# A two-block transformer on one core: expert retrieval merged with 42 down products, modulation sums turned to rows, compression with stationary blocks

## What is computed

```python
m  = (silu(c)     @ w_mod[l] + b_mod[l]).reshape(B, 9, 1024)     # tokens
mc = (silu(c_ctx) @ w_mod[l] + b_mod[l]).reshape(1, 9, 1024)     # context
x  = x + 0.5 * m[:, 2] * swiglu(mod_norm(x, m, 0, g), w1, w2)    # and the same for the 256 context tokens
...
```

```python
return gelu(blk @ w1 + b1) @ w2          # blk: 30 rows of 2048, w1: 2048 x 256
```

```python
q = (h @ w_q).reshape(B, TB, 8, 2, 128)              # 8 heads, 2 halves
s = einsum('btphd,phnd->btphn', q, subkeys)          # 128 subkeys each
v, i = top_k(s, 16)                                  # per head and half
cand = v[..., 0, :, None] + v[..., 1, None, :]       # 256 pair sums
tv, tj = top_k(cand, 16)                             # 16 experts a head
eidx = take_along_axis(cidx, tj);  w = softmax(tv)
a = gelu(einsum('btd,btpkd->btpk', hblk, w_down[eidx]))
return einsum('btpk,btpkd->btd', w * a, w_up[eidx])  # of 128 x 128 experts
```

## Time and profile before

| | |
|---|---|
| time, median of 3 runs | 3140.7 us (3140.38 to 3141.37) |
| the profiled execution | 3140.06 us |
| its span | 3138.3 us |
| granted TensorE clock, mean | 0.952 |
| PE / DVE / ACT / POOL busy | 2926.0 (93%) / 2188.5 (70%) / 1230.2 (39%) / 368.8 us (12%) |
| DMA | 450 MB, 143 GB/s over the span |

### The profile page before, as it was taken

One profiled execution on the slowest core, in us unless ns is written; L12 is line 12 of the kernel. 1 busy time (PEld: TensorE's weight loads), 2 busy tenths in 40 slices (PEclk: granted clock), 3 DMA queues, 4 the chain that ended last, 5 costly groups with the idle time before them and its releaser, 6 DMA issues. The chain is left out here.

```text
span 3138.3 us, 47109 instructions
## 1 busy us (share of the span) xinstructions
PE 2926.0 (93%) x16182; PEld 2491.5 (79%) x16182; DVE 2188.5 (70%) x4187; ACT 1230.2 (39%) x2276; POOL 368.8 (12%) x412
## 2 busy tenths in 40 slices
PE   7999999999999999999999997688379999999998
PEld 4888888568888888888859996568268999999997
DVE  2888894558888975657556664455998777777775
ACT  2322233443222332223455454154025454444454
POOL 0111115000111100100400000000375000000000
PEclk9999999999999999999999998689559999999999
DMA  5555442123544454534415556004002555555553
GB/s 230 175 174 192 171 146 94 41 101 132 190 175 169 148 200 148 174 132 159 130 36 170 185 173 229 1 27 149 1 0 73 186 186 186 186 187 186 187 187 120
DMA packets 107708, 450.01 MB, mean 143 GB/s; under 512 B 11953, under 2 KB 12593, under 8 KB 94257
## 3 DMA queue, kind: packets, MB, share of 16 engines
q1 hardware_dynamic: 93744, 347.46, 34.3%
q0 software_dynamic: 13824, 100.67, 8.5%
HBM read 447.04 MB, written 1.05 MB: 143 GB/s over the span
## 5 line engine op out<-in xcount | busy, mean ns | idle before, releaser
L177 DVE TENSOR_TENSOR weight_lo<-weight_ring,weight_hi 128x512 fp32r<-128x512 f32 x1272 | 942.0, 746 | 553.6 <-ACT weight_hi L170 539.1
L170 ACT ACTIVATE weight_hi<-weight_ring 128x512 fp32r<-128x512 f32 x1272 | 798.6, 631 | 1204.8 <-PE bank L256 1203.5
L254 PE MATMUL bank<-operand_hi,weight_hi 128*128 128x256 f32 (+1 forms) x3168 | 1042.7, 329 | 24.0 <-DVE operand_lo L591 12.9
L256 PE MATMUL bank<-operand_hi,weight_lo 128*128 128x256 f32 (+1 forms) x3168 | 1035.7, 327 | 0.0
L255 PE MATMUL bank<-operand_lo,weight_hi 128*128 128x256 f32 (+1 forms) x3168 | 1035.6, 327 | 0.0
L254 PEld LDWEIGHTS bank<-operand_hi,weight_hi 128*128 128x128 f32 x3168 | 604.0, 191 | 89.0 <-issue 21.4
L255 PEld LDWEIGHTS bank<-operand_lo,weight_hi 128*128 128x128 f32 x3168 | 604.2, 191 | 53.8
L256 PEld LDWEIGHTS bank<-operand_hi,weight_lo 128*128 128x128 f32 x3168 | 604.1, 191 | 51.2
L846 DVE SCALAR_TENSOR_TENSOR extension_ffn<-extension_ffn,silu_c 128x512 f32<-128x512 f32 x532 | 392.9, 788 | 1.7
L254 PE MATMUL bank<-hidden_hi_ffn,weight_hi 128*128 128x512 f32 (+1 forms) x704 | 258.5, 367 | 2.0 <-DVE arena L1071 1.9
L256 PE MATMUL bank<-hidden_hi_ffn,weight_lo 128*128 128x512 f32 (+1 forms) x704 | 255.7, 363 | 0.0
(11 more groups left out here) (253 smaller groups left out, 2934.3 us busy)
## 6 DMA issues: line engine op xcount, KB each, us to landing
weight_ring<-in_ffn SPq DMA_DIRECT2D x272, 512.0 KB, 3.6
weight_ring<-in_experts SPq DMA_DIRECT2D x256, 512.0 KB, 3.5
extension_ffn<-in_w_mods POOLq DMA_DIRECT2D x96, 1024.0 KB, 7.1
weight_ring<-in_w_mix SPq DMA_DIRECT2D x56, 512.0 KB, 3.6
weight_ring<-in_w_second SPq DMA_DIRECT2D x52, 512.0 KB, 3.9
extension_mixer<-in_rel_bias SPq DMA_DIRECT2D x2, 1536.0 KB, 6.7
arena<-in_x SPq DMA_DIRECT2D x1, 2048.0 KB, 9.2
arena<-in_cmp_k SPq DMA_DIRECT2D x1, 2048.0 KB, 11.6
```

What stands on the lines that cost most here:

```text
L170: nc.scalar.activation(self.hi[:, g % 2, h], self.ring[:, g % NS, h], ACT.Copy).then_inc(self.rounded, 1)
L177: self.nc.vector.tensor_tensor(self.lo[:, g % 2, h], self.ring[:, g % NS, h], self.hi[:, g % 2, h].bitcast(F32), ALU.subtract).then_inc(se ...
L254: nc.tensor.matmul(out, a_hi, b_hi, start=start and n == 0, stop=False)
L256: last = nc.tensor.matmul(out, a_lo, b_hi, start=False, stop=stop and n == len(pairs) - 1)
```

## The change

Three parts.

1. **Modulation sums in rows.** The accumulated tile now moves (512 columns), and the stationary operand is a window of 32 columns of `pick`, a matrix of zeros with one column of ones: the window's place decides in which of 32 rows of the bank the sum comes. At the end ScalarE copies the rows (`move`), TensorE transposes them in four pieces (`turn`), VectorE collects. Collecting and `finish` now stand behind the last product's VectorE work.
2. **Compression.** The 30 columns of the blocks are stationary and `w1` moves (256 columns), 32 fp32 matmuls; the result is copied, transposed and goes through gelu as before.
3. **Retrieval.** `Scores` and `stage_retrieve` become one class `Retrieve`, which also takes 42 down units (`K0`). The top 16 of a head begin when its scores are there. The tables are made for four tokens at a time (`BATCH`): VectorE's `compare` makes both tables in one instruction (128 x 4 x 2 x 128), GpSimd's `weigh` multiplies the first by the weights, `spread` is four matmuls, `keep` one copy of 128x512. `beside_down` places the batches: none in the first 19 units (`ALONE`), one per half unit in units 19 to 34, two per half in 35 to 41, four behind. The weights' subtraction is GpSimd's throughout this class (`subtract_beside`). The gelu of the 42 units is stored to device memory (`spill`) by SP's queue, and loaded again in `Experts`, whose order has 86 down units, and an up unit of a stored gelu after every second of the others and at the end.

```diff
+    def subtract_beside(self, pool, j, halves=(0, 1)):
+        g = self.g0 + j
+        for i in halves:
+            pool.wait_ge(self.rounded, 2 * g + i + 1)
+            h = slice(i * HALF, (i + 1) * HALF)
+            self.nc.gpsimd.tensor_tensor(self.lo[:, g % 2, h], self.ring[:, g % NS, h], self.hi[:, g % 2, h].bitcast(F32),
+                                         ALU.subtract).then_inc(self.split, 1)
...
         pe.wait_ge(self.halved.sem, self.halved.at(d + 1))
-        for n in range(self.blocks):
-            at = 2 * self.blocks * d + 2 * n
-            out = c.bank[6 + (d < self.early)][:, at:at + 2]
-            b = slice(n * P, (n + 1) * P)
-            nc.tensor.matmul(out, self.hi[:, b], c.ones_r[:, :], start=True, stop=False)
-            last = nc.tensor.matmul(out, self.lo[:, b], c.ones_r[:, :], start=False, stop=True)
+        for g in range(self.groups):
+            row = self.groups * d + g
+            pick = self.pick[:, ROWS - 1 - row:2 * ROWS - 1 - row]
+            out = c.bank[6 + (d < self.early)][0:ROWS, :]
+            final = d in (self.early - 1, self.n - 1) and g == self.groups - 1
+            nc.tensor.matmul(out, pick, self.hi[:, g * 512:(g + 1) * 512], start=(d in (0, self.early) and g == 0), stop=False)
+            last = nc.tensor.matmul(out, pick, self.lo[:, g * 512:(g + 1) * 512], start=False, stop=final)
         last.then_inc(self.summed.sem, 1)
...
             for n in range(2):
-                for m in range(2):
-                    for j in range(16):
-                        mm = nc.tensor.matmul(chip.bank[2 * n + m][:, 0:2 * NCB], w1[n][:, j, m * P:(m + 1) * P],
-                                              blk[n][:, j, :], start=(j == 0), stop=(j == 15))
-                    mm.then_inc(chip.product.sem, 1)
+                for j in range(16):
+                    mm = nc.tensor.matmul(chip.bank[n][0:2 * NCB, 0:256], blk[n][:, j, :], w1[n][:, j, :],
+                                          start=(j == 0), stop=(j == 15))
+                mm.then_inc(chip.product.sem, 1)
...
+NQ, K0 = 16, 42
+ALONE = 19
+TURN_AT, EXP_AT = [(ALONE - 1, 1), (ALONE + 14, 0)], [(ALONE - 2, 1), (ALONE + 13, 0)]
+LEFT = (P // BATCH + 4 * (K0 - ALONE - 16), S // BATCH)
...
+        def spread(b):
+            if b >= 4:
+                pe.wait_ge(self.kept.sem, self.kept.at(b - 3))
+            pe.wait_ge(self.weighted.sem, self.weighted.at(b + 1))
+            hots = self.hots(b)
+            for j in range(BATCH):
+                mm = nc.tensor.matmul(chip.bank[4 + b % 4][:, j * NK:(j + 1) * NK], hots[:, j, 0, :], hots[:, j, 1, :],
+                                      start=True, stop=True)
+            mm.then_inc(self.spread.sem, 1)
...
+        for i in range(K0):
+            if i < 2:
+                pe.wait_ge(self.evicted.sem, self.evicted.at(NQ - 1 + i))
+            else:
+                pe.wait_ge(self.gelu_done.sem, self.gelu_done.at(i - 1))
+            for half in range(2):
+                units.half_chunk(pe, NQ + i, half, chip.bank[i % 2][:, 0:S], x)
+                if i == 0 and half == 0:
+                    score(PH - 1)
+                for b in beside_down(i, half):
+                    spread(b)
+                if (i, half) == TURN_AT[1]:
+                    turn(1)
+            if (i, 1) == TURN_AT[0]:
+                turn(0)
...
+        for i in range(K0):
+            units.round(act, 0, NQ + i + 2, [0])
...
+            for b in beside_down(i, 0):
+                keep(b)
...
+            units.round(act, 0, NQ + i + 2, [1])
+            act.wait_ge(units.used, units.used_at(NQ + i))
+            if i >= 4:
+                act.wait_ge(chip.spilled[i % 4], 16 * (i // 4))
+            nc.scalar.activation(self.f[i % 4], chip.bank[i % 2][:, 0:S], ACT.Gelu_apprx_tanh).then_inc(self.gelu_done.sem, 1)
+            for b in beside_down(i, 1):
+                keep(b)
...
+        def weigh(b):
+            pool.wait_ge(self.compared.sem, self.compared.at(b + 1))
+            a = self.hots(b)[:, :, 0, :]
+            w = self.columns[:, 2, BATCH * b:BATCH * (b + 1)].unsqueeze(2).to_broadcast([P, BATCH, P])
+            nc.gpsimd.tensor_tensor(a, a, w, ALU.mult).then_inc(self.weighted.sem, 1)
+
+        for n in range(NQ):
+            units.subtract_beside(pool, n + 2)
+        for i in range(K0):
+            for half in range(2):
+                units.subtract_beside(pool, NQ + i + 2, [half])
+                for b in beside_down(i, half):
+                    weigh(b)
...
+def expert_order():
+    seq, early = [("down", K0), ("down", K0 + 1)], 0
+    for k in range(K0, NK):
+        seq.append(("up", k))
+        if k + 2 < NK:
+            seq.append(("down", k + 2))
+        if (k - K0) % 2 and early < K0:
+            seq.append(("up", early))
+            early += 1
+    return seq + [("up", k) for k in range(early, K0)]
...
-            run(nc, [add, Scores(chip, stream, add.then)])
-            stage_retrieve(chip)
-            stage_experts(chip, stream)
+            run(nc, [add, retrieve, Experts(chip, stream, retrieve)])
```

More of the change, by code:

```diff
@@ L790, in __init__ @@
         self.stepped = chip.mod_step.take(self.steps * self.n)
+        self.pick, self.rows = chip.extra["pick"], chip.part(A_RSTD, 512)[0:ROWS]
+        self.moved, self.turned = (s.take(1 + (early > 0)) for s in (chip.mod_moved, chip.mod_turned))
         self.rounded, self.halved, self.summed = (s.take(self.n) for s in (chip.mod_rounded, chip.mod_split, chip.mod_summed))
@@ new lines, in sum, with move, turn @@
+        last.then_inc(self.summed.sem, 1)
+    def move(self, act, upto):
+        c, nc = self.chip, self.chip.nc
+        act.wait_ge(self.summed.sem, self.summed.at(upto))
+        nc.scalar.activation(self.rows[:, :], c.bank[6 + (upto == self.early)][0:ROWS, :], ACT.Copy).then_inc(self.moved.sem, 1)
+    def turn(self, pe, upto):
+        c, nc = self.chip, self.chip.nc
+        pe.wait_ge(self.moved.sem, self.moved.at(1 if upto == self.early or not self.early else 2))
+        for k in range(4):
+            last = nc.tensor.transpose(c.bank[6 + (upto == self.early)][:, k * ROWS:(k + 1) * ROWS],
+                                       self.rows[:, k * P:(k + 1) * P], c.ident[0:ROWS, 0:ROWS])
+        last.then_inc(self.turned.sem, 1)
@@ L986, in tensor @@
                     work.sum(pe, d - 1)
+            if self.gate_first and n0 == 0:
+                work.turn(pe, work.early)
             for n in range(KT):
@@ L1001, in tensor @@
                     work.sum(pe, d - 1)
+        if work:
+            work.turn(pe, work.n)
     def scalar(self, act):
@@ L1019, in scalar @@
                     work.round(act, d - 1)
+                if self.gate_first and n0 == 0 and u == 13:
+                    work.move(act, work.early)
             if n0 + nh == FT:
@@ L1444, with beside_down @@
 E_HOT = E_WORK + 3 * S
-HOTS = 8
-B_WORDS = E_HOT + HOTS * 2 * P
+BATCH = 4
+B_WORDS = E_HOT + 2 * BATCH * 2 * P
+NQ, K0 = 16, 42
+ALONE = 19
+TURN_AT, EXP_AT = [(ALONE - 1, 1), (ALONE + 14, 0)], [(ALONE - 2, 1), (ALONE + 13, 0)]
+LEFT = (P // BATCH + 4 * (K0 - ALONE - 16), S // BATCH)
+def beside_down(i, half):
+    n = i - ALONE
+    if n < 0:
+        return range(0)
+    if n < 16:
+        return range(2 * n + half, 2 * n + half + 1)
+    first = P // BATCH + 4 * (n - 16) + 2 * half
+    return range(first, first + 2)
 class Proj:
@@ new lines, in __init__, with hots @@
+        n = S // BATCH
+        self.compared, self.weighted, self.spread, self.kept = (
+            x.take(n) for x in (chip.hot0, chip.hot1, chip.spread, chip.kept))
+        self.weight, self.columns = chip.part(0, S, NK), chip.part(E_SLOT, 3, S)
+        self.slots = chip.part(E_N, 3, SLOTS)
+        self.f = [chip.extra["early"][:, i, :] for i in range(4)]
+    def hots(self, b):
+        per = BATCH * 2 * P
+        at = b % 6 if b < S // BATCH - 8 else b % 2
+        if at < 2:
+            base = E_HOT + per * at
+        else:
+            base = (E_SC if b < P // BATCH else S * NK - 4 * per) + per * (at - 2)
+        return self.chip.part(base, BATCH, 2, P)
@@ L1894, in tensor @@
     def tensor(self, pe):
-        chip, nc, units, q, keys = self.chip, self.chip.nc, self.units, self.q, self.keys
+        chip, nc, units, r = self.chip, self.chip.nc, self.units, self.retrieve
         x = lambda kt: (self.hi[:, kt, :], self.lo[:, kt, :])
-        self.norm.sums(pe)
-        self.norm.spread(pe)
-        units.pair(pe, [chip.bank[0][:, 0:S], chip.bank[6][:, 0:S]], x, self.norm.split_in)
-        for n in range(2, 16):
-            k = n // 2
-            if n >= 4 and n % 2 == 0:
-                pe.wait_ge(self.evicted.sem, self.evicted.at(k - 1))
-            units.chunk(pe, 0, n, chip.bank[k % 2][:, n % 2 * S:(n % 2 + 1) * S], x)
@@ new lines, in tensor @@
+        pe.wait_ge(r.gelu_done.sem, r.gelu_done.at(K0))
+        pe.wait_ge(r.kept.sem, r.kept.at(S // BATCH))
+        w = 0
```

(13 more changed lines are left out.)

624 lines of the change are left out of this document (319 added, 305 removed).

## The result

| | before | changed |
|---|---|---|
| time, median | 3141.0 us (3140.4 to 3142.9, 4 runs) | 3220.1 us (3218.2 to 3222.3, 4 runs) |
| ratio, 95% interval | | 1.0251 (1.0233 to 1.0269) |
| the profiled execution, its span | 3140.1, 3138.3 us | 3220.8, 3219.0 us |
| granted TensorE clock, mean | 0.952 | 0.951 |

The change is 2.5% slower; 3213 us was forecast. Both early parts gain what they should, and the retrieval gives back more than that.

What follows compares the result with a forecast made beforehand. TensorE was taken to bound the feed-forward layers, waits between engines the rebuilt retrieval. 3140.1 + 112 (retrieval) - 28 (modulation sums) - 10.5 (compression) - 1 (block boundary) = 3212.6 us, 2.3% slower; range 3130 to 3245.

Steps and rivals of the forecast that it cites:

- Modulation sums: Feed-forward layers: 152 matmuls of 512 columns replace 608 of 2, gain 28 us, bounds 15 and 30.
- The deduction for VectorE's room: Modulation sums: 28 us taken of a 29.8 us gain, because VectorE has a little less room under the shorter cover.
- Compression: 32 matmuls with 256 moving columns replace 64 with 30: 17 us in place of 27.5, gain 10.5.
- The start of the region: From the first query product: TensorE waits 10 us, to 118; first comparison, weighting and copy end at 121 us.
- the ring: Units 19 to 34: half chunk, rounding, subtraction, weighting and spread follow without overlap, 6.1 us per half at full clock, 8.0 low.
- The clock: In the retrieval's loop: three halves of four at the low level, making 497 us from 427 at full clock.
- Region: First query product to first expert product behind the retrieval: 497 us, against 385 before, a cost of 112 us.
- Moved for nothing: 42 stores and loads on SP's queue and 42 early up units among the later units: no cost.
- the full clock through the ring: Rival: the full clock holds in the loop, region 427 us, 3142 us in all, no change; 10 in 100.
- The one in which the engines' sums count: Rival: GpSimd and its shared interface bound the halves, region 364, 3080 us; within the faster share, 16 in 100.

Runs made afterwards that it cites:

- the part alone: The kernel before with only the modulation sums in rows: 3110.9 us, ratio 0.9903 of before.
- 10.0 alone: The kernel before with only the compression part of the change: 3129.9 us, ratio 0.9965 of before.
- the dense run: The changed kernel with 12 unread fp32 matmuls on TensorE before each half unit's spread, from unit 20 on: 3166.5 us, ratio 1.0087 of before.
- the opened ring: The changed kernel with GpSimd's weighting of a half unit's batches before its subtraction: 3064.0 us, ratio 0.9759 of before.

## Why the prediction was right

By its own steps:

- **Modulation sums**: 28 taken, bound 30; the trace shows 30.4, the part alone 29.3. The deduction for VectorE's room was not needed, and the part gave what its matmuls alone were summed to, 29.8.
- **Compression**: 10.5 taken, 10.8 in the trace, 10.0 alone.
- **The start of the region**: TensorE's wait before the transposes was put at 10 us, to 118 us after the first query product, and is 11.66, to 122.7; the units before it took 111 us for 108, 1.5 of it behind a subtraction of GpSimd. The first batch was to be through at 121; its comparison began at 124.1 (2213.76), and its spread at 131.2 (2220.86), because GpSimd's first weighting already stands behind a subtraction that waits for TensorE: the ring begins one half unit earlier than it was counted.
- **The ring**: named with its edges, and each edge is in the timeline. At the full clock 6.1 us was summed, 5.75 is measured with TensorE kept dense. The term that was too long is GpSimd's weighting, taken at 1.30 from the subtraction's row, measured at 1.04. The estimate that the prediction set beside it from the Trainium skill's page GPSIMD Engine Reference, 1.1 us, is the nearer one for the weighting, and too low for the subtraction, 1.26. At the low clock 8.0 was summed; in this kernel's loop a half with one batch mostly lasts 6.9 to 7.8 us, with both levels in it, and 7.8 where the clock was nearest to low (0.51 to 0.55); six of the 32 last 8.4 to 9.3, and in each of these GpSimd's subtraction or weighting shows longer, beside VectorE's work.
- **The clock**: three halves of four at the low level were taken, a granted clock near 0.6. It was 0.69 to 0.72 in the halves with one spread and 0.80 to 0.81 in those with two. The first 32 halves took 243 us where 241 follow from the prediction, the 14 with two spreads 106 where 128 do; that is the term that was mis-sized, together with the last batches (11 us for 7). It comes from the second weighting, which costs 1.0 us by itself and in part runs beside the spread of the first, and from the higher clock.
- **Region**: 497 forecast, 487.1 measured. By its terms: 6 us more before the first half of the ring (127 for 121), 3 more in the halves with one spread, 22 less in those with two, 4 more at the end.
- **Moved for nothing**: the stores and loads cost nothing that the trace shows. The early up units did cost: the prediction said that TensorE needs 14 us for three ups and two downs and VectorE only 11, so TensorE sets the pace. It compared sums where a moment decides. An up unit's operands were made behind both subtractions of the unit's own weights, 0.1 us too late for TensorE, 128 times. This is the step that failed, by 19 to 20 us; the 10 us that the region fell short of its forecast hide half of it. That the result is within 7 us of the forecast is in so far luck; its sign and its mechanism, the ring, are not.
- **The rivals**: the full clock through the ring (3142) is what the dense run makes by force, 3166 with the late operands in it, so that rival's place and its price were right and it was not what the chip did. The one in which the engines' sums count (3080) is the opened ring: its 364 us for the region were 329. The estimate gave each of the 64 batches a subtraction, but 46 halves have one: 46 x 1.26 + 64 x (1.04 + 1.23) = 203 us behind the 124 of the start make 327, though the two kinds of halves each miss their share of it, as said of that run.

## What to carry to other kernels

When work is fitted between the steps of another loop, write down for one turn what each engine's instruction waits for and what stands ahead of it in its queue; if the line closes on itself within one turn, that sum of latencies is the pace, however little each engine has to do. Cut it at an edge, by doing first what is ready or by using a result one turn later: here either gave the same 156 us. Comparing the sums of two engines' work says which could be the bound, not whether an operand is ready in time; for an engine without idle time, look for a first instruction that is longer than its neighbours.

## What was not expected of the hardware

- A first matmul whose operand comes just as the unit before ends shows as a longer matmul and no idle time: 0.50 us in place of 0.39. The up unit is 0.12 us longer, 128 times, and the down unit ahead of it 0.07, 84 times.
- GpSimd's operation on two inputs of 128x512 takes 1.26 us when it subtracts and writes the rounded type, and 1.04 when it multiplies by a broadcast operand.
- A one-input cast of 128x128 on VectorE takes 0.23 us with GpSimd at rest and up to 1.36 beside it; a reduction of 128x2048 takes 2.29 in both. GpSimd's subtraction of 1.26 to 1.29 us takes up to 3.3 beside VectorE's two-input operations of 128x2048.
